# Suffix sums of a stick-breaking attention: two products of plain float32 become four of rounded high and low parts

## What is computed

```python
def stick_breaking_attention(q, k, v):
        z = jnp.einsum("bhqd,bhkd->bhqk", qs, k).astype(jnp.float32) * scale
        mask = kpos[None, :] < qpos[:, None]
        log_beta = jax.nn.log_sigmoid(z)
        log_one_minus = jnp.where(mask, jax.nn.log_sigmoid(-z), 0.0)
        suffix = lax.cumsum(log_one_minus, axis=3, reverse=True) - log_one_minus
        A = jnp.where(mask, jnp.exp(log_beta + suffix), 0.0)
        return jnp.einsum("bhqk,bhkd->bhqd", A.astype(v.dtype), v)
```

## Time and profile before

| | us |
|---|---|
| median of 3 runs | 744.69 (744.55 to 745.81) |
| the profiled execution | 744.59 |
| its span, first to last instruction | 742.8 |
| PE busy | 706.1 (95%) |
| DVE busy | 394.5 (53%) |
| ACT busy | 312.5 (42%) |
| HBM read | 200.59 MB, 271 GB/s over the span |

### The profile page before, as it was taken

The page is one execution under the profiler, slowest core; times in us unless marked ns, Lnnn a source line. Parts: engine busy times, 40 slices in busy tenths (PEclk is TensorE's granted clock), DMA queues, the critical chain, the costliest instruction groups (busy, mean ns, idle before and its releaser), DMA issues.

```text
span 742.8 us, 10290 instructions
## 1 busy us (share of the span) xinstructions
PE 706.1 (95%) x4050; PEld 488.7 (66%) x4050; DVE 394.5 (53%) x721; ACT 312.5 (42%) x529; POOL 2.6 (0%) x5
## 2 busy tenths in 40 slices
PE   5999999999999998999999999998999899999894
PEld 3999989777777766789977776764344343343342
DVE  5553744576847967533666568656233133323325
ACT  6553343655656546444457776432011021111113
POOL 1000000000000000000000000000000000000000
PEclk9999999999999999999999999999999999999998
DMA  9973766663653637667334433769999999999961
GB/s 355 415 295 143 269 255 236 232 226 116 227 199 140 240 135 306 243 263 288 114 114 157 172 125 114 269 234 424 422 426 421 427 430 430 419 429 426 418 280 56
DMA packets 19435, 202.18 MB, mean 272 GB/s; under 512 B 2370, under 2 KB 3138, under 8 KB 7364
## 3 DMA queue, kind: packets, MB, share of 16 engines
q1 hardware_dynamic: 18960, 201.00, 68.3%
q10 hardware_dynamic: 436, 0.65, 0.2%
HBM read 200.59 MB, written 1.05 MB: 271 GB/s over the span
## 4 chain that ended last, share of the span: by engine, by line
PE 50%; DMA 6%; DVE 4%; ACT 1%; issue 1%; DVEq 0%; ACTq 0%
PE psum L1206 11%; PE psum L854 7%; PE psum L1247 7%; PE psum L855 7%; PE psum L856 7%; DMA ring<-in_expert_w_down 6%; PE psum L1169 3%; PE psum L1152 2%; DVE ring_rounded L1756 1%; PE psum L1092 1%; PE psum L1117 1%; PE psum L1107 1%; PE psum L959 0%; DVE x_res L1612 0%; PE psum L1089 0%
## 5 line engine op out<-in xcount | busy, mean ns | idle before, releaser
L1756 DVE TENSOR_TENSOR ring_rounded<-ring,ring_rounded 128x1024 fp32r<-128x1024 f32 (+1 forms) x131 | 153.7, 1214 | 70.2 <-ACT ring_rounded L1439 70.0
L1439 ACT ACTIVATE ring_rounded<-ring 128x1024 fp32r<-128x1024 f32 (+1 forms) x132 | 130.0, 1039 | 9.8 <-PE psum L856 9.7
L854 PE MATMUL psum<-hT_rounded,ring_rounded 128*128 128x256 f32 x360 | 102.8, 286 | 0.0
L855 PE MATMUL psum<-work_rounded,ring_rounded 128*128 128x256 f32 x360 | 101.8, 283 | 0.0
L856 PE MATMUL psum<-hT_rounded,ring_rounded 128*128 128x256 f32 x360 | 101.8, 283 | 0.0
L855 PE MATMUL psum<-ring_rounded,hT_rounded 128*128 128x512 f32 (+1 forms) x224 | 86.5, 386 | 0.0
L1206 PE MATMUL psum<-ring,work 128*64 128x512 f32 x320 | 84.7, 594 | 0.3 <-issue 0.3
L854 PE MATMUL psum<-ring_rounded,hT_rounded 128*128 128x512 f32 (+1 forms) x208 | 83.1, 400 | 0.0
L856 PE MATMUL psum<-ring_rounded,work_rounded 128*128 128x512 f32 (+1 forms) x208 | 79.9, 384 | 0.0
L854 PEld LDWEIGHTS psum<-hT_rounded,ring_rounded 128*128 128x128 f32 x360 | 69.0, 192 | 3.0 <-issue 2.5
L855 PEld LDWEIGHTS psum<-work_rounded,ring_rounded 128*128 128x128 f32 x360 | 69.0, 192 | 0.1
(11 more groups left out here) (279 smaller groups left out, 1077.5 us busy)
## 6 DMA issues: line engine op xcount, KB each, us to landing
ring<-in_chunks SPq DMA_DIRECT2D x44, 2048.0 KB, 8.3
ring<-in_expert_w_down SPq DMA_DIRECT2D x16, 2048.0 KB, 19.1
ring<-in_expert_w_gate SPq DMA_DIRECT2D x12, 2048.0 KB, 19.9
ring<-in_expert_w_up SPq DMA_DIRECT2D x8, 2048.0 KB, 22.9
gates<-in_expert_w_up SPq DMA_DIRECT2D x4, 2048.0 KB, 26.2
hT<-in_expert_w_gate SPq DMA_DIRECT2D x4, 1024.0 KB, 20.0
mixed<-in_expert_w_gate SPq DMA_DIRECT2D x4, 1024.0 KB, 22.3
ring<-in_chunks SPq DMA_DIRECT2D x4, 512.0 KB, 8.0
```

Of the source, the lines that this page charges most:

```text
L854: nc.tensor.matmul(out, a[0], b[0], start=start, stop=False, skip_group_check=True)
L855: nc.tensor.matmul(out, a[0], b[1], start=False, stop=False, skip_group_check=True)
L1439: nc.scalar.activation(as_rounded(high_piece(c, q)), src[:, piece_of(c, q)], ACT.Copy).then_inc(chunk_hi, 1)
L1756: v.tensor_tensor(as_rounded(w[:, piece]), w[:, piece], was_rounded(high_piece(c, q)), ALU.subtract)\
```

## The change

`soft` of a head is split in a high part, `soft_high`, in the rounded type and a low part, the difference, also rounded. Both are multiplied by the same two matrices, which are copied once into the rounded type; zeros and ones are exact in it. So PE does four rounded products a head in place of two plain ones. DVE makes both parts: it writes the rounded sum, waits for it, writes the plain sum, and subtracts. `soft_high` lies in the tile `sig`, unused by then, and the two matrices in a free quarter of `mixed`. PE may begin with the high part when a new semaphore, `stick_high`, says so, and waits for `probs_ready` between the two parts.

```diff
@@ names
+        soft_high = sig[:, :, :].rearrange("p h n -> p (h n)")[:, 0:768].rearrange("p (b n) -> p b n", b=2)
+        suffix_rounded, ones_rounded = mixed[:, 2, 3, 0:P], mixed[:, 2, 3, P:T]
@@ PE, turn
-                    pe.wait_ge(probs_ready, h + 1)
                     if p < 12:
+                        pe.wait_ge(probs_ready, h + 1)
...
                     else:
 
-                        nc.tensor.matmul(b[:, 0:384], cs("suffix"), soft[:, h % 2, :], start=True, stop=False,
-                                         skip_group_check=True)
-                        last = nc.tensor.matmul(b[:, P:T], ones[:, 0:P], soft[:, h % 2, T:T + P], start=False, stop=True,
-                                                skip_group_check=True)
+                        pe.wait_ge(stick_high, h - 23)
+                        for z in (soft_high, soft):
+                            if z is soft:
+                                pe.wait_ge(probs_ready, h + 1)
+                            nc.tensor.matmul(b[:, 0:384], as_rounded(suffix_rounded), as_rounded(z[:, h % 2, :]),
+                                             start=z is soft_high, stop=False, skip_group_check=True)
+                            last = nc.tensor.matmul(b[:, P:T], as_rounded(ones_rounded), as_rounded(z[:, h % 2, T:T + P]),
+                                                    start=False, stop=z is soft, skip_group_check=True)
@@ DVE, probs
-                        z = soft[:, h % 2, :]
-                        v.scalar_tensor_tensor(z, s, 0.0, z, ALU.max, ALU.add).then_inc(probs_ready, 1)
+                        z, high = soft[:, h % 2, :], soft_high[:, h % 2, :]
+                        v.scalar_tensor_tensor(as_rounded(high), s, 0.0, z, ALU.max, ALU.add).then_inc(stick_high, 1)
+                        dve.wait_ge(stick_high, h - 23)
+                        link(v.scalar_tensor_tensor(z, s, 0.0, z, ALU.max, ALU.add))
+                        v.tensor_tensor(as_rounded(z), z, was_rounded(high), ALU.subtract).then_inc(probs_ready, 1)
@@ DVE, logf
+                dve.wait_ge(unit_done, UNITS.index(("proj", "a", 1, 1)) + 1)
+                v.tensor_copy(as_rounded(suffix_rounded), cs("suffix"))
+                v.tensor_copy(as_rounded(ones_rounded), ones[:, 0:P])
                 dve.wait_ge(fox_log, 1)
```

More of the change, by code:

```diff
@@ L600, in two_block_kernel @@
         stick_ready = sem("stick_ready")
+        stick_high = sem("stick_high")
         pt_evicted = sem("pt_evicted")
```

## The result

| | us |
|---|---|
| median before, 20 runs | 745.00 (744.55 to 745.81) |
| median after, 20 runs | 746.38 (745.11 to 747.21) |
| ratio after to before | 1.0016, 95% interval 1.0009 to 1.0023 |
| profiled execution after, its span | 746.90, 745.1 |
| forecast | 745.25 |

The account below looks back on a forecast made before the run. PE's hand-written order was taken to bound the kernel, with DVE 0.7 us behind; DVE's longer queue would turn PE's savings into idle time and add 0.66 us: 744.59 + 0.66 = 745.25 us, range 743.2 to 746.9.

Parts of the forecast that it names:

- What bounds: Stick-breaking heads 24 to 31: PE never idles, but DVE is a second bound 0.7 us behind it.
- What PE saves: PE's T steps, two heads each: 1.76 us becomes 1.12, saving 0.64 a pair, 2.6 us over four pairs.
- What DVE pays: Three dependent DVE instructions replace one: a head takes 1.73 us instead of 0.56, 9.4 us more over eight heads.
- Following the queue: DVE's delays followed through pairs 12 to 15: V(14) +0.32 us, T(15)'s end +0.6, expert loads and kernel end +0.7.
- T(15): PE's step for pair 15: comes at 442.36, waits for head 31's low part, starts the next unit at 444.3, +0.6 us.
- The prediction's own sign of being wrong: A granted clock under 1.00 between 436 and 448 us would make the clock the term left out.
- The fall of the clock: Rival: PE's idle time before V(14) or in T(15) brings 3.4 us at half clock; +0.9 to +2.3, chance 0.24.
- PE stays the bound: Rival: DVE's part of a pair fits behind ACT's, so all 2.6 us of PE's saving arrives; 742.0 us, chance 0.14.
- Hand-overs dearer: Rival: hand-overs or rounded outputs on DVE cost 0.07 us more each; +1.67, 746.3 us, chance 0.06.
- the change does not do what it says: Rival: rounded products cost as plain ones, so PE's T step doubles from 1.76 to 3.5 us; 751.6 us, chance 0.02.
- The rule on the semaphore: Skill rule that chained DVE instructions with semaphores cost nothing extra would give 744.25 us; the rows, with 0.03 each, give 745.25.
- the forecast's own band: Whole kernel: DVE's queue eats PE's gain, 744.2 to 745.9 us, chance 0.54.

Follow-up runs that it names:

- e1: The change with the low part left out: DVE makes one instruction a head, PE multiplies the high part twice; 743.36 us, ratio 0.9977 to the kernel before.
- e2: The change with PE's plain products of the kernel before, while DVE still makes its three instructions a head; 746.82 us, ratio 1.0020 to the kernel before.
- e8: Control: the kernel before, with the low part of the fourth quarter of weights f moved into DVE's step P(15); 745.03 us, ratio 0.9999.
- e3: The change plus two plain 128x512 products filling PE's idle time ahead of V(14); 745.63 us, ratio 1.0007 to the kernel before.
- e4: The change without DVE's wait between the high part and the plain sum; 744.76 us, ratio 0.9996 to the kernel before.
- e5: The change with one DVE low part (weights f, fourth quarter) moved from before step T(14) into idle time in P(15); 744.12 us, ratio 0.9989.
- e7: The change with both the wait of e4 left out and the low part of e5 moved; 743.76 us, ratio 0.9984 to the kernel before.

## Why the prediction was right, and what it left out

- **What bounds**: right. PE's own time counts only while DVE and ACT are ready first; e1, e2 and e8 show it from three sides.
- **What PE saves**: 1.76 to 1.12 was forecast, 1.20 measured, 0.56 saved a pair instead of 0.64. A 384- and a 128-column product take 0.29 together (433.15 and 433.44), 0.28 was taken; the first of the step takes 0.33 (432.82 and 433.15). That 0.28 comes so near is luck in part: the prediction had 0.17 and 0.11, the trace has 0.23 to the start of the 128 columns and 0.06 behind it.
- **What DVE pays**: right; starts 0.59 apart, as read from the pair in the earlier trace rows.
- **Following the queue**: right up to V(14). Shifted by 0.30, the copy came at 430.86 (430.99), L1843 of pair 14 at 436.87 (437.00), V(14) at 438.66 (438.66), heads 30 and 31 at 440.51 and 442.18 (440.54 and 442.21).
- **The step that failed**, though the total held, is T(15): "PE comes for T(15) at 442.36 ... and starts the next unit at 444.3". PE came at 443.89 and went on at 444.98 (both shifted), without a wait, for head 31's low part (done at 443.65 + 0.56 = 444.21 in after's own time) was there when it was wanted (444.99). V(14) and the first products of unit f00, up to 442.35, had run at half clock. Where e3 keeps the clock up, the next unit starts at 444.30, as forecast. The term left out of the sum is the clock's, and it is 0.6 to 0.7 us: +0.55 with DVE's queue alone (e3) and +0.72 for the difference make the +1.27 of the stretch, where the sum had +0.66. The prediction's own sign of being wrong, a granted clock under 1.00 between 436 and 448, came.
- **Rivals.** The fall of the clock, at 0.24, came together with the forecast's mechanism and not in its place; its price of +0.9 to +2.3 for the whole held the outcome. The prediction said that neighbours of dense products speak against a fall; they did not prevent it. *PE stays the bound* is out: DVE's part does not fit behind ACT's. Its price was also too high, since e1, with DVE out of the way, wins 2.06 and not 2.6. *Hand-overs dearer* and *the change does not do what it says* are out, by 0.59 and 1.20.
- **The rule on the semaphore.** A wait on DVE has a price: 0.59 between starts with it, 0.48 without (e4, where the increment stays and only the wait goes). By *VectorE: DVE Perf Modes* of the Trainium skill, "The DRAIN you can't avoid", chaining with a semaphore "costs nothing extra". The 0.11 saved in e4 speaks against it as the prediction read it, as a rule on the wait; on the increment alone no run here has a word. The profile after went by the rows: 0.59 between starts, and not 744.25.
- **Range and chances.** 746.38 lies between 743.2 and 746.9, and a change of 0.16% counts as within 0.2%, which had 0.64. But it lies outside the forecast's own band, 744.2 to 745.9 at 0.54: the range holds it because it was drawn out to the top of the clock's cases. It is also above 746.2, from where the prediction counted slower; that line was drawn from a before of 744.69, and the median before is 745.00 now.

## What to carry to other kernels

Before work is moved from the busiest engine to a less busy one, follow the second engine's queue to the next place where the first waits for it: the busy share (53% for DVE) didn't show what the slack at that place (0.7 us here) did. When the gain turns into idle time, look what stands in the queue ahead of the awaited instruction and is not yet wanted: moving one 1.2 us instruction won 1.9, more than the 1.27 that the change had lost. And a wait between two instructions of which neither needs the other's result cost 0.11 us each time here.

## What the runs showed of the hardware

- An idle time of 1.96 to 1.97 us of PE amid dense products was followed at once by 3.41 us at half clock, in both profiles of the change. Idle times of 1.46 and less at the same place (e1, e2, e4, e5, e7) were not, in one profile each.
- The length of the idle time alone does not settle it. Near 281 us PE stands 2.34 to 2.39 us in all ten profiles; in eight the clock fell there, in two (e3 and e5, both 2.34) it did not. And an idle time of 1.41 to 1.42, near 504 us before (ended by DVE, L1921) and a few us off in the others, was followed within 2 us by a fall in six profiles (before, the change twice, e1, e2, e5) and not in four (e3, e4, e7, e8). So the 1.46 of e4 is no safe length, and what else decides stays open. It also stays open whether those of the change's 20 runs that took 745.1 to 745.4 were executions without the fall at V(14); only the profiled ones have a trace, and the mean granted clock of a run does not tell them apart (0.989 to 0.992 for those four, 0.987 to 0.993 for the others).
- That fall near 281 costs nothing: with it PE waits 0.87 to 1.11 us for DVE at the first mark, without it 2.47 to 2.48, and goes on 17.3 to 17.4 us behind the first unit at 281 either way. In these two places, a half clock cost what no wait behind it covered.
